# First mixer: the head means from fp32r high and low parts of the squares

## The chip, the cores and the metric

The kernel runs on one core of one Trainium2 chip. The metric is the device time of one execution in microseconds, with the inputs and outputs in device memory. The core has a matrix engine (TensorE, here PE), VectorE (DVE), ScalarE (ACT), GpSimd (POOL) and queues for DMA transfers (SyncE, SP).

## The reference, cut to what matters

Three layers on 512 tokens of width 1024; the first one's mixer is concerned. `h` is the normed input, all in fp32:

```
z = h @ w_in -> gq, gk, gv, gr, glr, sq, sk, sv
# gated linear attention, 4 heads of 128 values
log_a = log_sigmoid(glr @ w_alpha2 + b_alpha) / 16
o_gla = rms_norm(gla_chunked(gq, gk, gv, log_a), gla_norm) * silu(gr)
# window attention, 8 heads of 64, 2 key heads
sq = rms_norm(sq, q_norm); sk = rms_norm(sk, k_norm)
o_swa = swa_sink_attention(sq, sk, sv, sinks)
x = x + concat(o_gla, o_swa) @ w_out
# rms_norm(x, g) = x * rsqrt(mean(x * x) + 1e-6) * g, the mean over one head
```

## The kernel before

Activations stand transposed, features on the 128 partitions and the 512 tokens along a row: a tile is 128x512. Each large product is made of three fp32r products: high parts, and high by low both ways. `three` issues them at lines 2054, 2055 and 2056. ScalarE makes a weight's high part (`split_hi`, line 858), VectorE its low part as the difference (`split_lo`, line 1396). A unit is the product for one tile of outputs: 8 blocks of 3 matmuls. In each engine the program is one stream of instructions in a fixed order; semaphores tie the streams together, and an engine that waits lets nothing past.

The first mixer (`mix_a`, one function for each engine) runs between the last 13 of the 19 units of the input projection. `beside` issues blocks of these units between the mixer's own products, on ACT and DVE the splits and the scaling of a finished unit (`evacuate`, line 1431). The mixer has a head part, and then 19 steps `k`, one for each pair of a head tile `t` and a query block `b` (16 pairs), and three to run out. In step `k` PE does the transposes of pair k-2 (line 2278), the products with the values of pair k-3 (2291), the odd work that the table `MISC_A` puts there, the scores of pair k+1 (2266), and 2 to 4 blocks. The scores wait until DVE has taken the row maxima (1805) of the pair before; the exponentials on ACT (1196) wait for the maxima; POOL scales.

Nine norms are made in this order: `NORMS = ["sk", "sq0", "sq1", "sq2", "sq3", 0, 1, 2, 3]`, numbers 0 to 8 below; the last four are those of the gated heads. For norm i:

- ACT: `squared(i)` (line 1140; for the gated heads line 1222, followed by a copy of the tile, 1224) writes the squares to `sq[:, i % 2, :]`.
- PE: `mean(i, bank)` (line 2252) multiplies them with a constant matrix: `blk64` (1/64 in the two blocks of a head) for i < 5, `ones` (1/1024) for the rest, so that each partition holds the mean of its head.
- ACT: `rooted` takes the logarithm (1148) and the exponential (1151), that is the reciprocal root.
- DVE: `normed` (1749) multiplies.

Operands of a mean are plain fp32. The trace holds two matmul records for each such product, one record for one of fp32r.

Means 0 and 1 stand ahead of the mixer's products for the gate (2359, whose result DVE takes at 1756), mean 2 after 20 further blocks, with six blocks and the first scores behind it. Mean 3 is in step 4, mean 4 in step 8, means 5 and 6 in step 9, means 7 and 8 in step 14. On DVE the head part has the decay's chain: three products of 128x1024 (1782, 1785, 1788) follow each other, the first waiting for an exponential of ACT (1177), and behind them come the scaling of a unit, a split and `normed(2)`. The products of line 2291 for a new head tile wait for the low part of the former one's output (`ol`, DVE line 1840), which is ordered behind the norms of its step.

Of the kernel before, what the change touches and what calls it, by code (L numbers as in the profile page):

```python
# [27 lines left out]
P = 128  # L28
S = 512
# [95 lines left out]
def build(nc, xT, vecs, conv, sinks, w_alpha2, pe, cmp_w1, cmp_w2, weights, yT, flow=FLOW):  # L125
# [6 lines left out]
    with ctx:  # L132
        def sb(name, shape, dt=f32, where=ctx):
            return where.enter_context(nc.sbuf_tensor(name, shape, dt))

        def sem(name):
# [7 lines left out]
        hhi = sb("hhi", [P, KD * S], f32r)  # L144
        hlo = sb("hlo", [P, KD * S], f32r)
        rstd = sb("rstd", [P, S])
        sq = sb("sq", [P, 3, S])
        sumsq = sq[:, 2, :]
        ident = sb("ident", [P, P])
# [50 lines left out]
        fcA = sb("fcA", [P, 32], f32, ma)  # L200
        pT = sb("pT", [P, 2, 2, 2, P], f32, ma)
        rst2 = sb("rst2", [P, 2, S], f32, ma)
        ma.close()

        mb = ExitStack()
# [80 lines left out]
        stored = sem("stored")  # L286

        A = {k: sem("a_" + k) for k in (
            "svT", "svT_c", "nsq", "nms", "nln", "nrstd", "nq", "bias", "zero", "logit", "logit_b", "lsig",
            "decay", "rest", "eb", "enb", "ed", "qe", "ke", "kd", "kdT_c", "masked", "gvT_c", "st", "oc",  # L290
            "misc", "s", "m", "p", "rec", "scaled", "t", "tc", "pv", "sig", "og", "ohi", "olo")}
        B = {}
# [98 lines left out]
        def wlow(n):  # L391
# [6 lines left out]
            if n in KEPT:  # L398
# [32 lines left out]
        MISC_A_NO = {(kind, i): n for n, (kind, i) in enumerate((m[1], m[2]) for m in MISC_A if m[1] != "nm")}  # L431

        def arow(name):
            return tile(zsq, int(name[2])) if name[:2] == "sq" else tile(za, ROW_A[name])
# [393 lines left out]
        def _(act):  # L828
# [302 lines left out]
            def mix_a():  # L1131
                p = "in_a"

                def squared(i):

                    name = NORMS[i]
                    if i >= 2:
                        act.wait_ge(A["nms"], i - 1)
                    act.wait_ge(evac[p], UNIT_A[name] + 1)
                    act.activation(sq[:, i % 2, :], arow(name), ACT.Square).then_inc(A["nsq"], 1)  # L1140

                def rooted(i, bank):

# [8 lines left out]

                squared(0)
                squared(1)
                rooted(0, 4)
                rooted(1, 5)
                act.wait_ge(A["svT"], 1)
# [23 lines left out]
                for k in range(STEPS_A):  # L1181
                    if 0 <= k - 2 < len(PAIRS_A):
                        j = k - 2
                        n = min(PAIRS_A[j][1] + 1, 2)
                        if j >= 2:

                            act.wait_ge(A["pv"], j - 1)
                        act.wait_ge(A["t"], j + 1)
                        act.activation(pT[:, j % 2, :, 2 - n:2, :],
                                       ps[:, 2 + j % 2, :].rearrange("p (g j q) -> p g j q", g=2, q=P)[:, :, 2 - n:2, :],  # L1190
                                       ACT.Copy).then_inc(A["tc"], 1)
                    for s in (2 * k, 2 * k + 1) if k < len(PAIRS_A) else []:
                        w = P * min(PAIRS_A[k][1] + 1, 2)
                        part = pA[:, s % 6, 2 * P - w:2 * P + 1]
                        act.wait_ge(A["m"], s + 1)
                        act.activation(part, part, ACT.Exp, scale=-1.0, bias=nmA[:, s:s + 1], accum_out=smA[:, s:s + 1]
                                       ).then_inc(A["p"], 1)
                    for u in ended(p, k):
                        beside(p, u)
                    if k >= 6 and k % 4 == 2:  # L1200

                        t = k // 4 - 1
                        act.wait_ge(A["pv"], 4 * t + 4)
                        act.activation(tile(oh, 4 + t), ps[:, 4, :], ACT.Copy).then_inc(A["ohi"], 1)
                    if k == 3:
                        squared(3)
                    if k == 7:
                        squared(4)
                    for kind, i, banks in misc_a_at(k):
                        if kind in ("kt", "gv", "o"):  # L1210
                            act.wait_ge(A["misc"], MISC_A_NO[kind, i] + 1)
                        if kind == "kt":
                            act.activation(tile(kdT, i), ps[:, banks[0], :], ACT.Copy).then_inc(A["kdT_c"], 1)
                        if kind == "gv":
                            act.activation(tile(gvT, i), ps[:, banks[0], :], ACT.Copy).then_inc(A["gvT_c"], 1)
                        if kind == "nm":
                            rooted(i, banks[0])
                        if kind == "o":
                            for hh in range(2):
                                h = 2 * i + hh  # L1220
                                act.wait_ge(A["nms"], 4 + h)
                                act.activation(sq[:, (5 + h) % 2, :], ps[:, banks[hh], :], ACT.Square).then_inc(A["nsq"], 1)
                                act.wait_ge(A["gvT_c"], h + 1)
                                act.activation(tile(za, ZGV + h), ps[:, banks[hh], :], ACT.Copy).then_inc(A["oc"], 1)
                for u in finished_at(p, STEPS_A - 1):
# [166 lines left out]
        def _(dve):  # L1392
# [343 lines left out]
            def mix_a():  # L1736
                p = "in_a"

                def normed(i):
# [7 lines left out]
                    else:  # L1747
                        dve.wait_ge(evac[p], UNIT_A[name] + 1)
                    dve.scalar_tensor_tensor(out=out, in0=out, scalar=col(gain), in1=rst2[:, i % 2, :],
                                             op0=ALU.mult, op1=ALU.mult).then_inc(A["nq"], 1)  # L1750

                gk, gq = za[:, ZGK * S:ZGK * S + 2 * S], za[:, ZGQ * S:ZGQ * S + 2 * S]
                dve.wait_ge(ld_vec, 48)
                for t in range(2):
# [16 lines left out]
                for t in range(2):  # L1771
# [15 lines left out]
                dve.wait_ge(evac[p], UNIT_A["gq1"] + 1)  # L1787
                dve.scalar_tensor_tensor(out=gq, in0=gq, scalar=HD ** -0.5, in1=eb[:, :], op0=ALU.mult,
                                         op1=ALU.mult).then_inc(A["qe"], 1)
                beside(p, 9)  # L1790
                dve.wait_ge(evac[p], 10)
                dve.memset(ps[:, 0:2, 2 * P:2 * P + 1], 0.0).then_inc(A["zero"], 1)
# [3 lines left out]
                for k in range(STEPS_A):  # L1796
# [12 lines left out]
                    if 0 <= k - 1 < len(PAIRS_A):  # L1809
                        j = k - 1  # L1810

                        dve.wait_ge(A["p"], 2 * j + 2)
                        dve.reciprocal(fcA[:, 2 * j:2 * j + 2], smA[:, 2 * j:2 * j + 2]).then_inc(A["rec"], 1)
                    for u in ended(p, k):
                        evacuate(p, u, 0)
                    for kind, i, banks in misc_a_at(k):
# [19 lines left out]
                    if k >= 6 and k % 4 == 2:  # L1836

                        t = k // 4 - 1
                        dve.wait_ge(A["ohi"], t + 1)
                        dve.tensor_tensor(tile(ol, 4 + t), ps[:, 4, :], tile(oh, 4 + t).bitcast(f32), ALU.subtract  # L1840
                                          ).then_inc(A["olo"], 1)
                    for u in ended(p, k):
                        n = FIRST[p] + u + 2
                        split_lo(n, 0)
# [205 lines left out]
        def _(pe_):  # L2050
# [195 lines left out]
            def mix_a():  # L2246
                p = "in_a"

                def mean(i, bank):

                    pe_.wait_ge(A["nsq"], i + 1)
                    pe_.matmul(ps[:, bank, :], blk64[:, :] if i < 5 else ones[:, :], sq[:, i % 2, :], start=True, stop=True
                               ).then_inc(A["nms"], 1)

                def scores(k):

# [484 lines left out]
```

## Time and profile before

| | |
|---|---|
| median of 3 runs | 1655.83 us (1655.77 to 1656.39) |
| profiled execution, time | 1656.2 us |
| its span, first to last instruction | 1654.5 us |
| PE busy | 1626.6 us (98%), 8090 matmul records |
| DVE busy | 878.7 us (53%) |
| ACT busy | 709.3 us (43%) |
| POOL busy | 181.4 us (11%) |

The head part of the first mixer runs from about 49 to 76 us of the span, its steps to about 170 us. Times in the rows are microseconds from the span's start. A timeline merges instructions of one line; where it names a mean duration or several records, the start is that of the first. Matmul ends are modelled and overlap the next start, so a matmul's cost is read from start to start. A bracket tells how long the engine sat idle before and which instruction ended that.

### The profile page before, as it was taken

What the parts mean: (1) busy time and instruction counts of PE and PEld (TensorE: products, weight loads), DVE (VectorE), ACT (ScalarE), POOL (GpSimd) and SP (SyncE); (2) the same over time, 40 slices, a digit from 0 to 9 for tenths busy, and PEclk for the clock granted to TensorE, in tenths of its full rate; (3) what the DMA queues carried; (4) which work ended last, traced back from release to release, by engine and by line L of the source; (5) the groups of instructions that cost most, each with busy time, mean ns of one, the idle gap of its engine ahead of it and who ended that gap; (6) DMA issues with size and microseconds to landing.
All of it is one profiled execution on the core that took longest, in us unless ns stands there. A gap on an engine that the chain in (4) does not pass through costs nothing.

```text
span 1654.5 us, 22402 instructions
## 1 busy us (share of the span) xinstructions
PE 1626.6 (98%) x8090; PEld 1350.5 (82%) x8090; DVE 878.7 (53%) x1472; ACT 709.3 (43%) x1210; POOL 181.4 (11%) x257
## 2 busy tenths in 40 slices
PE   8999999999999999999899999999999999999997
PEld 7777788888888888888787888888898888888887
DVE  5634567777743356666756544443238644444233
ACT  4545454444432226676756332232237522323231
POOL 2012000000000032444513000002001200000001
PEclk9999999999999999999999999999999999999999
DMA  5211223322333252121112323233331232333331
GB/s 182 88 41 39 90 89 102 101 89 92 98 102 102 90 130 71 45 65 52 52 61 81 95 96 101 90 101 97 94 115 53 64 101 89 101 95 95 102 102 52
DMA packets 57158, 144.87 MB, mean 88 GB/s; under 512 B 14160, under 2 KB 20976, under 8 KB 57088
## 3 DMA queue, kind: packets, MB, share of 16 engines
q1 hardware_dynamic: 55680, 141.58, 27.4%
q0 software_dynamic: 688, 1.26, 0.4%
q10 hardware_dynamic: 720, 1.10, 0.2%
q8 instruction: 44, 0.72, 0.2%
q14 instruction: 26, 0.21, 0.0%
HBM read 138.67 MB, written 2.10 MB: 85 GB/s over the span
## 4 chain that ended last, share of the span: by engine, by line
PE 93%; ACT 3%; DVE 2%; issue 1%; POOL 0%; DVEq 0%; ACTq 0%; POOLq 0%
PE ps L2054 26%; PE ps L2055 26%; PE ps L2056 26%; PE ps L2155 1%; PE ps L2153 1%; PE ps L2154 1%; PE ps L2223 1%; PE ps L2467 1%; PE ps L2452 1%; PE ps L2505 1%; PE ps L2453 1%; PE ps L2213 1%; PE ps L2626 0%; PE ps L2291 0%; PE ps L2266 0%
## 5 line engine op out<-in xcount | busy, mean ns | idle before, releaser
L2054 PE MATMUL ps<-hhi,whi 128*128 128x512 f32 x1392 | 549.4, 395 | 0.6 <-DVE hlo L2010 0.4
L2056 PE MATMUL ps<-hhi,wlo 128*128 128x512 f32 x1392 | 543.0, 390 | 0.0
L2055 PE MATMUL ps<-hlo,whi 128*128 128x512 f32 x1392 | 543.0, 390 | 0.0
L1396 DVE TENSOR_TENSOR wlo<-raw,whi 128x1024 fp32r<-128x1024 f32 x226 | 276.8, 1225 | 444.6 <-ACT whi L858 441.6
L858 ACT ACTIVATE whi<-raw 128x1024 fp32r<-128x1024 f32 x239 | 252.8, 1058 | 512.1 <-PE ps L2056 512.0
L2054 PEld LDWEIGHTS ps<-hhi,whi 128*128 128x128 f32 x1392 | 261.9, 188 | 62.8 <-issue 8.2
L2056 PEld LDWEIGHTS ps<-hhi,wlo 128*128 128x128 f32 x1392 | 261.7, 188 | 55.3
L2055 PEld LDWEIGHTS ps<-hlo,whi 128*128 128x128 f32 x1392 | 262.0, 188 | 53.3 <-issue 1.2
L2054 PE MATMUL ps<-ahi,whi 128*128 128x512 f32 x432 | 168.0, 389 | 0.0
L2055 PE MATMUL ps<-alo,whi 128*128 128x512 f32 x432 | 168.0, 389 | 0.0
L2056 PE MATMUL ps<-ahi,wlo 128*128 128x512 f32 x432 | 168.0, 389 | 0.0
L923 ACT ACTIVATE ahi<-gated 128x512 f32 (+1 forms) x66 | 41.7, 632 | 148.1 <-DVE gated L1519 148.1
L1490 DVE TENSOR_TENSOR pre<-ps,rstd 128x512 f32<-128x512 f32 x132 | 90.0, 683 | 21.7 <-ACT rstd L1080 14.0
L2054 PEld LDWEIGHTS ps<-ahi,whi 128*128 128x128 f32 x432 | 81.1, 188 | 16.9
L2056 PEld LDWEIGHTS ps<-ahi,wlo 128*128 128x128 f32 x432 | 81.1, 188 | 16.9
L2055 PEld LDWEIGHTS ps<-alo,whi 128*128 128x128 f32 x432 | 81.1, 188 | 16.7
L1521 DVE TENSOR_TENSOR alo<-gated,ahi 128x512 f32 (+1 forms) x66 | 45.7, 692 | 59.3 <-ACT ahi L923 59.3
L1302 ACT ACTIVATE pth<-ps 128x128 fp32r<-128x128 f32 (+3 forms) x96 | 36.7, 433 | 40.3 <-PE ps L2467 39.7
L717 POOL DMA_DIRECT2D cw<-cmp_w x4 | 3.4, 854 | 419.8 <-PE ps L2056 419.8
L1957 DVE TENSOR_TENSOR ptl<-ps,pth 128x128 fp32r<-128x128 f32 (+3 forms) x96 | 42.9, 485 | 11.9 <-ACT pth L1302 11.6
L1412 DVE TENSOR_TENSOR sq<-sq 128x512 f32<-128x512 f32 x42 | 28.9, 688 | 35.6 <-ACT sq L896 25.8
L912 ACT ACTIVATE cvt<-pre,convw 128x512 f32<-128x512 f32 x44 | 35.4, 807 | 28.8 <-DVE pre L1490 28.8
(381 smaller groups left out, 2083.7 us busy)
## 6 DMA issues: line engine op xcount, KB each, us to landing
raw<-w_up_b SPq DMA_DIRECT2D x88, 512.0 KB, 3.4
raw<-w_up_a SPq DMA_DIRECT2D x44, 512.0 KB, 3.5
raw<-w_in_b SPq DMA_DIRECT2D x23, 512.0 KB, 3.5
raw<-w_in_a SPq DMA_DIRECT2D x19, 512.0 KB, 3.5
raw<-w_down_b SPq DMA_DIRECT2D x16, 512.0 KB, 3.5
raw<-w_out_a SPq DMA_DIRECT2D x8, 512.0 KB, 3.5
raw<-w_down_a SPq DMA_DIRECT2D x8, 512.0 KB, 3.5
raw<-w_out_b SPq DMA_DIRECT2D x8, 512.0 KB, 3.4
```

The lines of the kernel that those rows point to most:

```text
L858: act.activation(whigh(n), raw_of(n), ACT.Copy).then_inc(hi_done, 1)
L912: act.activation(cvt[:, s, :], pre[:, s, :], ACT.Identity, bias=convw[:, bass.ds(3 * 2 * KF + c + fi, 1)], scale=convw[:, bass.ds(2 * 2 * ...
L923: act.activation(tile(ahi, f + fi), gated[:, :], ACT.Copy).then_inc(k["ahi"], 1)
L1302: act.activation(pth[:, j % 2, 0:n, s % 2, :], ps[:, 2 + s % 2, 0:n * P].rearrange("p (j q) -> p j q", q=P), ACT.Copy).then_inc(B["hi"], 1)
L1396: dve.tensor_tensor(wlow(n), raw_of(n), whigh(n).bitcast(f32), ALU.subtract).then_inc(lo_done, 1)
L1412: dve.tensor_tensor(sumsq[:, :], sumsq[:, :], sq[:, m % 2, :], ALU.add).then_inc(sq_used, 1)
L1490: dve.tensor_tensor(pre[:, u % 2, :], ps[:, u % 4, :], rstd[:, :], ALU.mult).then_inc(evac[p], 1)
L1521: dve.tensor_tensor(tile(alo, f + fi), gated[:, :], tile(ahi, f + fi).bitcast(f32), ALU.subtract).then_inc(k["alo"], 1)
L1957: dve.tensor_tensor(ptl[:, j % 2, 0:n, s % 2, :], ps[:, 2 + s % 2, 0:n * P].rearrange("p (j q) -> p j q", q=P), pth[:, j % 2, 0:n, s % 2, ...
L2054: pe_.matmul(out, wh, hi, start=start, stop=False)
L2055: pe_.matmul(out, wh, lo, start=False, stop=False)
L2056: return pe_.matmul(out, wl, hi, start=False, stop=stop)
```

## The change

Each mean's squares are written twice by ACT: as fp32, and as fp32r (`sqr`), the high part. DVE subtracts the two and writes the low part as fp32r (`sq_low`) over the fp32 squares, whose memory it shares. PE multiplies high and low part with an fp32r copy of the constant, in two accumulating products in place of one fp32 product. ACT makes the two fp32r constants (`blk64r`, `onesr`) once. The means wait for the low part (semaphore `nql`) in place of the squares (`nsq`). The order of the means on PE is unchanged. DVE's `squared_low(i)` is put into its stream at fixed places: 0 and 1 at the start of the mixer, 2 behind the third of the three long products (`qe`), 5 in step 8 ahead of the unit's scaling, and 3, 4, 6 and 7 with 8 at steps 3, 7, 8 and 13, each ahead of that step's `split_lo`.

```diff
@@ -144,6 +144,9 @@
         hhi = sb("hhi", [P, KD * S], f32r)
         hlo = sb("hlo", [P, KD * S], f32r)
         rstd = sb("rstd", [P, S])
+        over_sq = ExitStack()
+        sq_low = sb("sq_low", [P, 2, S], f32r, over_sq)
+        over_sq.close()
         sq = sb("sq", [P, 3, S])
         sumsq = sq[:, 2, :]
         ident = sb("ident", [P, P])
@@ -200,6 +203,8 @@
         fcA = sb("fcA", [P, 32], f32, ma)
         pT = sb("pT", [P, 2, 2, 2, P], f32, ma)
         rst2 = sb("rst2", [P, 2, S], f32, ma)
+        sqr = sb("sqr", [P, 2, S], f32r, ma)
+        means = sb("means", [P, 2 * P], f32r, ma)
         ma.close()
 
         mb = ExitStack()
@@ -286,7 +291,7 @@
         stored = sem("stored")
 
         A = {k: sem("a_" + k) for k in (
-            "svT", "svT_c", "nsq", "nms", "nln", "nrstd", "nq", "bias", "zero", "logit", "logit_b", "lsig",
+            "svT", "svT_c", "nsq", "nqh", "nql", "nconst", "nms", "nln", "nrstd", "nq", "bias", "zero", "logit", "logit_b", "lsig",
             "decay", "rest", "eb", "enb", "ed", "qe", "ke", "kd", "kdT_c", "masked", "gvT_c", "st", "oc",
             "misc", "s", "m", "p", "rec", "scaled", "t", "tc", "pv", "sig", "og", "ohi", "olo")}
         B = {}
@@ -429,6 +434,14 @@
                   (9, "nm", 5, [7]), (9, "nm", 6, [5]), (10, "gv", 3, [7]), (11, "cs", 1, [5, 7]),
                   (13, "o", 1, [5, 7]), (14, "nm", 7, [5]), (14, "nm", 8, [7])]
         MISC_A_NO = {(kind, i): n for n, (kind, i) in enumerate((m[1], m[2]) for m in MISC_A if m[1] != "nm")}
+
+        def square_hi(i):
+            return sqr[:, i % 2, :]
+
+        def square_lo(i):
+            return sq_low[:, i % 2, :]
+
+        blk64r, onesr = means[:, 0:P], means[:, P:2 * P]
 
         def arow(name):
             return tile(zsq, int(name[2])) if name[:2] == "sq" else tile(za, ROW_A[name])
@@ -1138,6 +1151,7 @@
                         act.wait_ge(A["nms"], i - 1)
                     act.wait_ge(evac[p], UNIT_A[name] + 1)
                     act.activation(sq[:, i % 2, :], arow(name), ACT.Square).then_inc(A["nsq"], 1)
+                    act.activation(square_hi(i), arow(name), ACT.Square).then_inc(A["nqh"], 1)
 
                 def rooted(i, bank):
 
@@ -1152,6 +1166,9 @@
 
                 squared(0)
                 squared(1)
+                act.wait_ge(const_a, 1)
+                act.activation(blk64r, blk64[:, :], ACT.Copy).then_inc(A["nconst"], 1)
+                act.activation(onesr, ones[:, :], ACT.Copy).then_inc(A["nconst"], 1)
                 rooted(0, 4)
                 rooted(1, 5)
                 act.wait_ge(A["svT"], 1)
@@ -1220,6 +1237,7 @@
                                 h = 2 * i + hh
                                 act.wait_ge(A["nms"], 4 + h)
                                 act.activation(sq[:, (5 + h) % 2, :], ps[:, banks[hh], :], ACT.Square).then_inc(A["nsq"], 1)
+                                act.activation(square_hi(5 + h), ps[:, banks[hh], :], ACT.Square).then_inc(A["nqh"], 1)
                                 act.wait_ge(A["gvT_c"], h + 1)
                                 act.activation(tile(za, ZGV + h), ps[:, banks[hh], :], ACT.Copy).then_inc(A["oc"], 1)
                 for u in finished_at(p, STEPS_A - 1):
@@ -1749,6 +1767,15 @@
                     dve.scalar_tensor_tensor(out=out, in0=out, scalar=col(gain), in1=rst2[:, i % 2, :],
                                              op0=ALU.mult, op1=ALU.mult).then_inc(A["nq"], 1)
 
+                def squared_low(i):
+
+                    dve.wait_ge(A["nsq"], i + 1)
+                    dve.wait_ge(A["nqh"], i + 1)
+                    dve.tensor_tensor(square_lo(i), sq[:, i % 2, :], square_hi(i).bitcast(f32), ALU.subtract
+                                      ).then_inc(A["nql"], 1)
+
+                squared_low(0)
+                squared_low(1)
                 gk, gq = za[:, ZGK * S:ZGK * S + 2 * S], za[:, ZGQ * S:ZGQ * S + 2 * S]
                 dve.wait_ge(ld_vec, 48)
                 for t in range(2):
@@ -1787,6 +1814,7 @@
                 dve.wait_ge(evac[p], UNIT_A["gq1"] + 1)
                 dve.scalar_tensor_tensor(out=gq, in0=gq, scalar=HD ** -0.5, in1=eb[:, :], op0=ALU.mult,
                                          op1=ALU.mult).then_inc(A["qe"], 1)
+                squared_low(2)
                 beside(p, 9)
                 dve.wait_ge(evac[p], 10)
                 dve.memset(ps[:, 0:2, 2 * P:2 * P + 1], 0.0).then_inc(A["zero"], 1)
@@ -1811,6 +1839,8 @@
 
                         dve.wait_ge(A["p"], 2 * j + 2)
                         dve.reciprocal(fcA[:, 2 * j:2 * j + 2], smA[:, 2 * j:2 * j + 2]).then_inc(A["rec"], 1)
+                    if k == 8:
+                        squared_low(5)
                     for u in ended(p, k):
                         evacuate(p, u, 0)
                     for kind, i, banks in misc_a_at(k):
@@ -1839,6 +1869,8 @@
                         dve.wait_ge(A["ohi"], t + 1)
                         dve.tensor_tensor(tile(ol, 4 + t), ps[:, 4, :], tile(oh, 4 + t).bitcast(f32), ALU.subtract
                                           ).then_inc(A["olo"], 1)
+                    for i in {3: [3], 7: [4], 8: [6], 13: [7, 8]}.get(k, []):
+                        squared_low(i)
                     for u in ended(p, k):
                         n = FIRST[p] + u + 2
                         split_lo(n, 0)
@@ -2248,9 +2280,11 @@
 
                 def mean(i, bank):
 
-                    pe_.wait_ge(A["nsq"], i + 1)
-                    pe_.matmul(ps[:, bank, :], blk64[:, :] if i < 5 else ones[:, :], sq[:, i % 2, :], start=True, stop=True
-                               ).then_inc(A["nms"], 1)
+                    pe_.wait_ge(A["nconst"], 2)
+                    pe_.wait_ge(A["nql"], i + 1)
+                    weight = blk64r if i < 5 else onesr
+                    pe_.matmul(ps[:, bank, :], weight, square_hi(i), start=True, stop=False)
+                    pe_.matmul(ps[:, bank, :], weight, square_lo(i), start=False, stop=True).then_inc(A["nms"], 1)
 
                 def scores(k):
 
```

## Rows read from the trace of the kernel before

**Rows 1.** The page: chain that ended last, share of the span by engine.

```profile
PE 93%; ACT 3%; DVE 2%; issue 1%; POOL 0%; DVEq 0%; ACTq 0%; POOLq 0%
```

**Rows 2.** Timeline of PE, 46 to 58 us: start us, us, engine line, count.

```profile
49.44 1.88 PE L2252 MATMUL ps<-sq,blk 128*128 128x512 f32 x4
51.26 1.12 PE L2359 MATMUL ps<-za,wal 16*128 16x512 f32 x2
52.31 0.50 PE L2054 MATMUL ps<-hhi,whi 128*128 128x512 f32 x1
52.64 0.40 PE L2055 MATMUL ps<-hlo,whi 128*128 128x512 f32 x1
52.88 0.39 PE L2056 MATMUL ps<-hhi,wlo 128*128 128x512 f32 x1
```

**Rows 3.** Timeline of PE, 62 to 76 us.

```profile
70.33 1.02 PE L2252 MATMUL ps<-sq,blk 128*128 128x512 f32 x2
...
71.42 0.40 PE L2055 MATMUL ps<-hlo,whi 128*128 128x512 f32 x1
```

**Rows 4.** Timeline of DVE, 36 to 76 us.

```profile
69.85 1.23 DVE L1782 TENSOR_TENSOR kd<-za,kd 128x1024 f32<-128x1024 f32 x1 [0.78 <-ACT kd L1177]
...
73.46 0.68 DVE L1431 TENSOR_TENSOR za<-ps,rstd 128x512 f32<-128x512 f32 x1
```

**Rows 5.** Timeline of PE, 104 to 134 us.

```profile
118.86 1.12 PE L2252 MATMUL ps<-sq,blk 128*128 128x512 f32 x2
119.92 0.70 PE L2266 MATMUL ps<-za,zsq 64*128 64x256 f32 x4
...
131.95 0.70 PE L2266 MATMUL ps<-za,zsq 64*128 64x256 f32 x4 [0.42 <-DVE nmA L1805]
```

**Rows 6.** Timeline of PE, 142 to 184 us.

```profile
153.18 1.98 PE L2252 MATMUL ps<-sq,ones 128*128 128x512 f32 x4
...
158.62 0.44 PE L2291 MATMUL ps<-pT,svT 128*64 128x128 f32 x4
```

**Rows 7.** Timeline of ACT, 36 to 76 us.

```profile
50.50 0.69 ACT L1148 ACTIVATE rst<-ps,epsc 128x512 f32<-128x512 f32 x1 [4.58 <-PE ps L2252]
...
66.81 0.61 ACT L1140 ACTIVATE sq<-zsq 128x512 f32<-128x512 f32 x1
...
68.76 1.06 ACT L1177 ACTIVATE kd<-kd 128x1024 f32<-128x1024 f32 x1 [0.38 <-DVE kd L1774]
```

**Rows 8.** Timeline of ACT, 142 to 184 us.

```profile
150.42 0.60 ACT L1222 ACTIVATE sq<-ps 128x512 f32<-128x512 f32 x1 [1.93 <-PE ps L2340]
...
151.39 0.60 ACT L1222 ACTIVATE sq<-ps 128x512 f32<-128x512 f32 x1
...
153.04 0.50 ACT L1196 ACTIVATE pA<-pA,nmA 128x257 f32<-128x257 f32 x1
```

**Rows 9.** Timeline of DVE, 142 to 184 us.

```profile
148.53 1.22 DVE L1396 TENSOR_TENSOR wlo<-raw,whi 128x1024 fp32r<-128x1024 f32 x1 [2.36 <-ACT whi L858]
150.89 0.43 DVE L1805 CUSTOM_DVE_ANT_0 pA<-ps,biasA 128x257 f32<-128x257 f32 x1 [1.14 <-PE ps L2266]
...
157.79 0.68 DVE L1840 TENSOR_TENSOR ol<-ps,oh 128x512 fp32r<-128x512 f32 x1
```

**Rows 10.** Waits, 44 to 165 us: total, times, longest us.

```profile
DVE la L1756 <- PE ps L2359: 9.5, 2, 6.4
```

**Rows 11.** Timeline of ACT, 104 to 134 us.

```profile
120.03 0.60 ACT L1222 ACTIVATE sq<-ps 128x512 f32<-128x512 f32 x1 [4.21 <-PE ps L2252]
```

**Rows 12.** Timeline of DVE, 104 to 134 us.

```profile
123.64 0.75 DVE L1749 SCALAR_TENSOR_TENSOR zsq<-zsq,vec,rst 128x512 f32<-128x512 f32 x1 [8.06 <-ACT rst L1151]
124.31 0.42 DVE L1805 CUSTOM_DVE_ANT_0 pA<-ps,biasA 128x257 f32<-128x257 f32 x1
```

**Rows 13.** Windows of 20 us: busy us by engine, PEclk, DMA share, GB/s.

```profile
640.00:660.00 20.00, 18.71 (x90) 15.59 (x91) 12.31 (x46) 12.29 (x38) 9.87 (x13) 0.83 0.21 53
```

**Rows 14.** Waits of PE over the whole span.

```profile
PE ps L2452 <- DVE nmB L1941: 5.8, 16, 1.4
PE ps L2189 <- POOL ident L680: 4.6, 1, 4.6
```

## Prediction

> **What bounds the kernel now.** I read the page first: which engine the chain that ended last runs over. It is TensorE (PE) for 93% [rows 1]: what takes a matmul off PE is worth its time, unless an operand comes late. The change sits in the first mixer, so I then read the timelines of PE, ScalarE (ACT) and VectorE (DVE) from 44 to 170 us side by side. The reader is to see three things there. A mean costs PE two half-rate passes [rows 2, 3]. Mean 2 stands on PE at 70.33, long before DVE is through with the long products of the gates, the first at 69.85 [rows 3, 4]. And at two places PE waits for DVE: before the scores at 131.95 (0.42 us idle) and before the products at 158.62 [rows 5, 6], each after a mean whose root runs over ACT and DVE. Anything put on ACT or DVE ahead of these is on the path.
>
> **Prices.** From mean 2's start to that of the second product after it are 1.09 us; one product is 0.24 (52.64 to 52.88), so an f32 mean holds PE 0.86 [rows 2, 3]. Products of fp32r start 0.23 to 0.24 apart, the first behind f32 work 0.33 [rows 2]. So the new pair costs 0.33 + 0.23 = 0.56. Means 0 and 1 took 1.82 (49.44 to 51.26); now 0.33 + 3 x 0.23 = 1.02, and up to 0.1 for the way back to f32: saved 0.75. Mean 2 saves 0.30. A mean inside the loop took 1.06 to the next score (118.86 to 119.92) [rows 5]; 0.2 of that may be the scores' own weight load and stay: saved 0.3 to 0.5, I take 0.4. The pairs 5, 6 and 7, 8 save about 0.8 each. Everything together is 0.75 + 0.30 + 2 x 0.4 + 2 x 0.8 = 3.45 us, if nothing waits. The second square holds ACT 0.49 (150.42 to 151.39 is a square and a copy) [rows 8]. A subtraction is of the form of line 1840, 0.68 long, and holds DVE 0.61, half of the 1.22 of a 128x1024 one [rows 9].
>
> **Means 0 and 1: a gain.** Squares, copies of the constants and subtractions fall before 49.44. ACT stood idle 4.58 us before the root at 50.50, and DVE up to 6.4 us for the products of line 2359 [rows 7, 10]. The two extra squares and two copies (128 columns each, at most a square) need 4 x 0.49 = 2.0 us, two subtractions 2 x 0.61 = 1.2 us: hidden. Without that cover they would cost their own length, 3.2 us. The products of line 2359 start 0.75 early, and DVE's additions, which waited for them, go with them; so does all that hangs on them up to 70 us.
>
> **Mean 2: a wait.** ACT does the second square behind the one at 66.81. Behind it are queued two exponentials; the later, at 68.76, had 0.38 us of idle time before it [rows 7] and comes 0.05 to 0.15 late against its old distance, and DVE's product at 69.85 waits for it [rows 4]. The subtraction is put behind the third long product. DVE was free of that at 73.46 [rows 4]; now 73.46 - 0.75 + 0.05 = 72.76, and the low part is there at 72.76 + 0.68 + 0.05 = 73.49. PE comes to the mean at 70.33 - 0.75 = 69.58 and stands 3.9 us, with nothing else allowed past. Queued behind it are 18 products and all of the loop. Mean 2 starts 3.16 late and saves 0.30: PE is 2.86 late. ACT and DVE gain slack, PE alone sets the pace from there, so nothing takes this back.
>
> **Mean 3.** The subtraction in step 3 stands before the unit's split and waits for ACT; the split used to wait for the unit's high part alone, and two squares and a subtraction now lie between: 0.49 + 0.60 + 0.61 = 1.7 us, and the row maxima behind the split are as much later. PE asks for these only behind 12 products (2.8 us at 0.23), transposes and the mean, so I cost it at nothing; without that cover it is up to 1.7. PE: 2.86 - 0.4 = 2.46 late. Subtraction 4 (step 7) has the same form and DVE idle around it; subtraction 5 too.
>
> **Steps 8 to 10: a dearer chain.** From mean 4 to the scores at 131.95 the chain left PE: square and copy on ACT (120.03, released by the mean), exponentials, the root, line 1749 on DVE at 123.64, maxima at 124.31, and again ACT and DVE up to the scores [rows 5, 11, 12]. The mean now ends 0.40 earlier (0.33 + 0.39 against 1.12 long), the second square adds 0.49, subtraction 6 stands between 123.64 and 124.31 and adds 0.60: +0.69. What means 4, 5 and 6 save on PE is lost in the wait at these scores. PE: 2.46 + 0.69 = 3.15 late.
>
> **Steps 13 and 14: a new wait.** ACT has square 150.42, second square, copy, square, second square: the last starts at 150.42 + 4 x 0.485 = 152.36 and ends at 152.96. DVE's subtraction 8 waits for it (153.0 to 153.6). Queued behind are the split of line 1396, which was at 148.53, now 153.6 to 154.75, and the maxima of pair 14, at 150.89 before, now 154.75 [rows 8, 9]. The exponentials need these: 154.75 + 0.43 + 0.01 = 155.19 in place of 153.04, 2.15 late [rows 8]. Everything after them on ACT and DVE, the two roots, line 1749 twice and line 1840 at 157.79, was a gapless chain from there to the products at 158.62, which had just been waiting for it: 2.15 late [rows 6, 9]. Mean 7 and 8 themselves (153.18) have their operands within 0.1 us, and their 0.8 is lost in the wait. PE: 3.15 + 2.15 = 5.3 late, and what follows is released by PE.
>
> **Sum.** Profiled execution: 1654.5 span and 1.7 around it, 1656.2. With +5.3: 1661.5. The median of the runs shown is 0.4 below the profiled one, so I forecast 1661.1 us. Own range: mean savings 0.3 or 0.5 each, subtraction held at 0.59 to 0.69, the exponential 0.05 or 0.15 late: 1660.2 to 1662.2.
>
> **The clock.** Between 640 and 660 us the clock granted to PE was 0.83 on the mean, with PE busy 18.71 of 20 us [rows 13]: it stood at the lower of its two levels (1.2 of 2.4 GHz) for a part of them. (1 - 0.83) x 20 = 3.4 us of full clock were lost, without a long wait there. Outside the start, the longest wait of PE for another engine in the whole trace is 1.4 us [rows 14]; the new one is 3.9. The fall costs between nothing and 3.4 us. I take nothing, because dense products stand on both sides of the wait, and price the other as a rival. The Trainium skill (TensorE: Matmul & The Clock Gate, section "Why this matters for your kernels") says that a long idle gap between bursts of matmuls drops the clock; by that rule the fall comes in this wait, against this change; the trace has a fall, but no such wait to show it by.
>
> **Rivals.** *The clock falls in the wait for mean 2.* For: the row above, where less brought it down. Against: the dense work around it. A loss of 3.4 is a low stretch of 6.8 us; what of it lies in the wait is free, at most 3.9, so (6.8 - 3.9) / 2 = 1.5 to 3.4 is left, about 2.3: 1663.4. *The later fall goes away.* The fall near 640 us came without a long wait, so the same work 5 us later may not bring it. Up to 3.4 comes back, less what DVE's and ACT's own chains held up there anyway; I take 2.3: 1661.1 - 2.3 = 1658.8, no measurable change. *Only mean 2's wait counts.* If ACT's and DVE's additions in steps 8 to 14 are covered after all, PE is 2.86 late and gets up to 2 x 0.4 + 2 x 0.8 = 2.4 back: 1656.3 to 1658.7, no change. Against: chains without gaps. *Faster.* The one mechanism is that the subtractions come in time, so that the two passes fewer are PE's gain: 1655.83 - 3.45 = 1652.4. It decides at mean 2: DVE would have to reach subtraction 2 at 68.9 in place of 72.76, and this needs three 1.1 us products out of its way; they are in its queue, in order.
>
> **Chances.** Forecast 0.55; clock falls in the wait 0.22; later fall gone 0.10; only mean 2 0.09; faster 0.04. About 0.2%, 3.3 us, is what a measurement of this kernel can tell from no change: 1652.5 to 1659.1. So slower 0.80 (forecast, clock, a part of the others), same 0.16, faster 0.04. The range takes the first three in: 1658.3 to 1664.6.
>
> **What would show it.** PE idle some 3.9 us before line 2252's third mean, released by DVE's subtraction; if it is under 1 us, the step on mean 2 is wrong. Nine new pairs at about 0.23 to 0.33 apart in place of 18 half-rate passes. Idle PE of 1.5 to 2 us before the scores of step 10 and before the products of step 15, where 0.42 and next to nothing were; DVE's split and maxima of step 13 behind a subtraction that waits for ACT. Granted clock 1.00 from 60 to 180 us. Behind 180 us the same sequence, 5.3 us later. The prediction is wrong if the clock moves by more than 2 us in sum, or if the loop absorbs one of the three delays.

## The result, and the profile after

The changed kernel takes 1664.60 us (median of 5 runs, 1663.74 to 1665.13) against 1655.83 us (1655.54 to 1656.39): the ratio is 1.0055, 95% interval 1.0044 to 1.0065, so 7 to 11 us slower. Forecast were 1661.1 and at most 1664.6. The profiled execution has a span of 1662.0 us, 7.5 more than before.

The page of the changed kernel, its first part and the chain by engine, answering to [rows 1]:

```profile
PE 1625.7 (98%) x8090; PEld 1351.2 (81%) x8090; DVE 884.4 (53%) x1481; ACT 713.6 (43%) x1221; POOL 181.0 (11%) x257
...
PE 92%; ACT 3%; DVE 3%; issue 2%; POOL 0%; DVEq 0%; ACTq 0%; POOLq 0%
```

PE is busy 0.9 us less than before (1625.7 against 1626.6) in a span that is 7.5 longer, so it stands still 8.4 us more. The busy time alone does not show the clock: cheaper means and slower products are both in it. The waits of PE over the whole span say where it stands (engine and line, waited for; total, times, longest, in us); of [rows 14] the start's 4.6 and the second mixer's are still there, and three lines are new or grown, by 8.3 us together (the second one was 0.4 before):

```profile
PE ps L2286 <- DVE sq_low L1774: 4.2, 2, 3.8
PE ps L2300 <- DVE nmA L1833: 2.7, 2, 1.7
PE ps L2325 <- DVE ol L1870: 1.8, 1, 1.8
```

Timeline of PE around mean 2, answering to [rows 3]. Lines 2086 to 2088 are the three products of a block, 2286 and 2287 the mean's pair, 2300 the scores:

```profile
69.44 0.39 PE L2088 MATMUL ps<-hhi,wlo 128*128 128x512 f32 x1
73.67 0.47 PE L2286 MATMUL ps<-sqr,means 128*128 128x512 f32 x1 [3.84 <-DVE sq_low L1774]
73.97 0.39 PE L2287 MATMUL ps<-sq_low,means 128*128 128x512 f32 x1
...
74.93 0.63 PE L2086 MATMUL ps<-hhi,whi 128*128 128x512 f32 x1
75.36 0.63 PE L2087 MATMUL ps<-hlo,whi 128*128 128x512 f32 x1
...
80.03 0.49 PE L2300 MATMUL ps<-za,zsq 64*128 64x128 f32 x4
```

The last product before the mean starts at 69.44; PE then sits idle 3.84 us until DVE's subtraction. The pair starts 0.30 apart and costs what the fp32r products around it do. From 74.9 the same products start 0.43 apart, not 0.23. DVE in the same stretch, answering to [rows 4]:

```profile
69.23 1.23 DVE L1809 TENSOR_TENSOR kd<-za,kd 128x1024 f32<-128x1024 f32 x1 [0.80 <-ACT kd L1194]
...
71.70 1.22 DVE L1815 SCALAR_TENSOR_TENSOR za<-za,eb 128x1024 f32<-128x1024 f32 x1
72.84 0.68 DVE L1774 TENSOR_TENSOR sq_low<-sq,sqr 128x512 fp32r<-128x512 f32 x1
```

The subtraction (line 1774) stands behind the long products and starts at 72.84. Windows of the changed kernel (us; PE, PEld, DVE, ACT and POOL busy, then the granted clock):

```profile
72.00:76.00 4.00, 2.33 (x8) 1.92 (x9) 3.52 (x6) 1.32 (x2) 0.00 (x0) 0.86 0.00 0
76.00:80.00 4.00, 4.00 (x13) 2.90 (x12) 0.54 (x1) 0.00 (x0) 0.00 (x0) 0.72 0.40 131
164.00:168.00 4.00, 2.19 (x10) 1.70 (x11) 2.28 (x8) 1.86 (x6) 1.47 (x3) 0.88 0.00 0
168.00:172.00 4.00, 4.00 (x21) 2.89 (x20) 0.69 (x1) 1.33 (x2) 0.69 (x2) 0.70 0.00 0
640.00:660.00 20.00, 18.92 (x102) 15.78 (x100) 12.03 (x46) 11.95 (x38) 5.09 (x8) 0.91 0.20 52
```

The clock is below 1 in every row. Before, it was 1.00 in the first four of these windows and 0.83 in the last [rows 13]. At (1 - clock) x length, 1.68 us of full clock are lost at each of the first two places (0.56 + 1.12, and 0.48 + 1.20); at 640 us 1.8 are lost where it was 3.4.

The two places in the loop, PE, answering to [rows 5, 6]:

```profile
123.09 0.50 PE L2286 MATMUL ps<-sqr,means 128*128 128x512 f32 x1
...
123.74 0.70 PE L2300 MATMUL ps<-za,zsq 64*128 64x256 f32 x4
...
136.87 0.70 PE L2300 MATMUL ps<-za,zsq 64*128 64x256 f32 x4 [1.68 <-DVE nmA L1833]
```

```profile
158.13 0.50 PE L2286 MATMUL ps<-sqr,means 128*128 128x512 f32 x1
...
160.60 0.70 PE L2300 MATMUL ps<-za,zsq 64*128 64x256 f32 x4 [1.03 <-DVE nmA L1833]
...
165.81 0.44 PE L2325 MATMUL ps<-pT,svT 128*64 128x128 f32 x4 [1.83 <-DVE ol L1870]
...
168.26 0.63 PE L2086 MATMUL ps<-hhi,whi 128*128 128x512 f32 x1
```

The scores of step 10 wait 1.68 us for the row maxima, the products of step 15 1.83 for the low part of line 1870. DVE and ACT in steps 13 and 14, answering to [rows 8, 9]:

```profile
158.03 0.69 DVE L1774 TENSOR_TENSOR sq_low<-sq,sqr 128x512 fp32r<-128x512 f32 x1 [0.78 <-ACT sqr L1240]
158.63 1.22 DVE L1414 TENSOR_TENSOR wlo<-raw,whi 128x1024 fp32r<-128x1024 f32 x1
159.77 0.42 DVE L1833 CUSTOM_DVE_ANT_0 pA<-ps,biasA 128x257 f32<-128x257 f32 x1
...
164.99 0.68 DVE L1870 TENSOR_TENSOR ol<-ps,oh 128x512 fp32r<-128x512 f32 x1
```

```profile
157.29 0.63 ACT L1240 ACTIVATE sqr<-ps 128x512 fp32r<-128x512 f32 x1
...
160.23 0.51 ACT L1213 ACTIVATE pA<-pA,nmA 128x257 f32<-128x257 f32 x1 [1.54 <-DVE nmA L1833]
```

DVE waits 0.78 us for ACT's second square (157.29), subtracts, splits, and only then takes the maxima for which the exponential at 160.23 has waited 1.54.

Start of the same work in both profiled executions, from the timelines of PE (ACT for the loading of the Silu table):

| work | before | after | later by |
|---|---|---|---|
| mean 0 | 49.44 | 49.50 | 0.06 |
| mean 2 | 70.33 | 73.67 | 3.34 |
| first scores | 75.40 | 80.03 | 4.63 |
| mean 4 | 118.86 | 123.09 | 4.23 |
| scores in step 10 | 131.95 | 136.87 | 4.92 |
| mean 7 | 153.18 | 158.13 | 4.95 |
| products in step 15 | 158.62 | 165.81 | 7.19 |
| Silu table on ACT | 171.30 | 180.10 | 8.80 |
| first compression product, second mixer | 626.7 | 635.5 | 8.8 |
| end | 1654.5 | 1662.0 | 7.5 |

### The profile page after: what moved, and what is told of

Its sections match the earlier page's. It is cut to its first block, busy times and chain, and to the rows that moved or that the text cites. A ratio compares the mean times of both kernels' runs of the same rounds, so it can differ in the third digit from the quotient of the medians.

```text
span 1662.0 us, 22433 instructions
## 1 busy us (share of the span) xinstructions
PE 1625.7 (98%) x8090; PEld 1351.2 (81%) x8090; DVE 884.4 (53%) x1481; ACT 713.6 (43%) x1221; POOL 181.0 (11%) x257
## 4 chain that ended last, share of the span: by engine, by line
PE 92%; ACT 3%; DVE 3%; issue 2%; POOL 0%; DVEq 0%; ACTq 0%; POOLq 0%
PE ps L2086 26%; PE ps L2087 25%; PE ps L2088 25%; PE ps L2187 1%; PE ps L2185 1%; PE ps L2186 1%; PE ps L2255 1%; PE ps L2501 1%; PE ps L2486 1%; PE ps L2539 1%; PE ps L2487 1%; PE ps L2245 1%; PE ps L2660 0%; PE ps L2325 0%; PE ps L2300 0%
```

## The experiments

Ten kernels were run, each against the kernel before on the same chip; the medians of that kernel there were 1655.73 (first four), 1655.76 (next four) and 1656.21 us (last two). One profile was taken of each. Where a profile and the median of its kernel tell different things, both are given: two executions of one kernel can differ by 1 to 3 us.

### Subtraction 2 ahead of the long products

```diff
                 dve.memset(state[:, :, 0, :], 0.0).then_inc(A["st"], 1)
+                squared_low(2)
                 dve.wait_ge(A["ed"], 1)
...
-                squared_low(2)
                 beside(p, 9)
```

> Subtraction 2 moved ahead of the three long products, into DVE's idle 0.8 us. Theory A (waits and clock falls): the wait for mean 2 (3.84 us) is gone and with it the clock fall behind it; PE is 1.05 us early at the first scores where it was 4.63 late, 0.8 early at the scores of step 10, 1.5 late at the products of step 15; with or without the second fall (1.7) and the changed fall near 640 us: 1657 to 1660 us. Theory B (only the wait counts, the clock loss comes anyway): 1664.6 - 3.9 = 1660.7 or more. Theory C (means were slow in themselves): near 1664.

Measured: 1659.78 us (1657.41 to 1661.11), ratio 1.0021 (1.0012 to 1.0031). PE's timeline around the mean and the first scores, and DVE's behind the moved subtraction:

```profile
70.51 0.39 PE L2286 MATMUL ps<-sqr,means 128*128 128x512 f32 x1
...
75.58 0.49 PE L2300 MATMUL ps<-za,zsq 64*128 64x128 f32 x4 [0.32 <-DVE ps L1820]
```

```profile
70.03 1.23 DVE L1810 TENSOR_TENSOR kd<-za,kd 128x1024 f32<-128x1024 f32 x1 [0.26 <-ACT kd L1194]
```

No wait before the pair. This execution started its mixer 0.86 later than the one before (50.30 against 49.44 for mean 0), so the first scores at 75.58 are 0.68 early, not 1.05: they wait 0.32 for DVE's zeroing (line 1820). The moved subtraction did not delay that: the first long product behind it still waits 0.26 for ACT. The zeroing itself comes 0.67 earlier, counted from mean 0 (25.17 behind it, before 25.84), but PE comes 1.0 earlier. Behind it everything went as in the changed kernel: 1.68 us of wait at step 10, 1.81 at step 15, and the clock fell there alone (0.79 in 160 to 164 and in 164 to 168 us). One place of one instruction was worth 4.8 us of 8.8. Theory B (1660.7 or more) is out by the windows, where the first fall is gone; the time, 0.9 us below it, would not rule it out, since its interval reaches 1660.9.

### The wait for mean 2 filled

```diff
                 pe_.wait_ge(A["nln"], 1)
+                for n in range(16):
+                    pe_.matmul(ps[:, 4, :], blk64r, square_hi(1), start=True, stop=True)
                 mean(2, 4)
```

> Sixteen products of 128x512 without use (3.6 us) fill the wait for mean 2; nothing else is changed. Theory A: the wait stays as long, the clock does not fall behind it: 1.7 us less, about 1662.9 (1662.2 to 1663.6). Theory B (the fall has another cause, or costs nothing): no change from 1664.6, granted clock below 1 near 75 us again.

Measured: 1662.64 us (1660.73 to 1664.59), ratio 1.0038 (1.0024 to 1.0053). Windows of this kernel, from an execution of 1664.2 us:

```profile
76.00:80.00 4.00, 4.00 (x20) 3.04 (x19) 1.27 (x5) 0.38 (x2) 0.00 (x0) 1.00 0.39 131
...
136.00:140.00 4.00, 4.00 (x14) 2.88 (x11) 1.45 (x6) 1.33 (x4) 1.95 (x4) 0.60 0.40 128
...
168.00:172.00 4.00, 4.00 (x20) 2.91 (x19) 0.69 (x1) 1.11 (x2) 1.03 (x2) 0.64 0.00 0
```

The clock stays at 1.00 after mean 2, which itself is no earlier (74.08, 4.20 behind the filling's start at 70.08). The first scores start 3.42 later than before, with mean 0 0.44 later: 2.98 by the change, against 4.57 without the filling. So the fall behind this wait is from PE standing still in it, and costs 1.6 us. The rows show this and the time alone does not: its interval overlaps that of the changed kernel (1.0044 to 1.0065). In this execution it fell at 137 us instead, behind the wait of step 10, where it had not in the changed kernel's profile.

### Subtractions 7 and 8 behind the maxima

```diff
-                    for i in {3: [3], 7: [4], 8: [6], 13: [7, 8]}.get(k, []):
+                    for i in {3: [3], 7: [4], 8: [6]}.get(k, []):
...
                     if k == 8:
                         squared_low(5)
+                    if k == 14:
+                        squared_low(7)
+                        squared_low(8)
```

> Subtractions 7 and 8 moved from step 13 to step 14, behind the row maxima of pair 14. Theory A: the split and the maxima are back in time, the chain to the products of step 15 is 0.6 late for the two squares of ACT in place of 2.2; the wait of 1.83 us there shrinks to about 1.4, the second fall is gone or not: 1.6 to 3.3 less, 1661.3 to 1663.0. Theory B (that chain is bound by the squares on ACT alone): 1664 to 1665.

Measured: 1662.54 us (1660.15 to 1662.85), ratio 1.0033 (1.0018 to 1.0047). DVE's timeline:

```profile
154.17 1.23 DVE L1414 TENSOR_TENSOR wlo<-raw,whi 128x1024 fp32r<-128x1024 f32 x1 [2.36 <-ACT whi L871]
156.53 0.43 DVE L1833 CUSTOM_DVE_ANT_0 pA<-ps,biasA 128x257 f32<-128x257 f32 x1 [1.14 <-PE ps L2303]
...
158.72 0.76 DVE L1774 TENSOR_TENSOR sq_low<-sq,sqr 128x512 fp32r<-128x512 f32 x1 [0.74 <-ACT sqr L1240]
...
164.01 0.69 DVE L1873 TENSOR_TENSOR ol<-ps,oh 128x512 fp32r<-128x512 f32 x1
```

Split and maxima wait for nobody's square any more. From mean 7 to the products of step 15 are 6.01 us (158.83 to 164.84); they were 5.44 before and 7.68 in the changed kernel: +0.57 and +2.24. The wait is 1.17 us, and no fall followed it. The fall at mean 2 was larger in this execution:

```profile
72.00:76.00 4.00, 2.40 (x6) 1.95 (x7) 3.25 (x5) 1.14 (x2) 0.00 (x0) 0.50 0.00 0
76.00:80.00 4.00, 4.00 (x14) 3.14 (x13) 0.75 (x1) 0.18 (x1) 0.00 (x0) 0.65 0.39 131
```

That is 3.4 us of clock lost in place of 1.7, with a wait of 3.81 us. So the time falls into theory A's range, but what was saved at step 15 (1.67 by the rows, and the 1.7 of the fall) is partly hidden by the other fall.

### A wait alone, in the kernel before

```diff
                 pe_.wait_ge(A["nln"], 1)
+                pe_.wait_ge(A["qe"], 1)
                 mean(2, 4)
```

> The kernel before, where mean 2 on PE also waits for the third long product of DVE (nothing of the change in it). Theory A: wait of 3.1 us at mean 2 and a clock fall of 1.7 behind it, then up to 1.3 given back or taken near 640 us: 1659 to 1662, likeliest 1660.6. Theory B (a wait does not bring the clock down): 1658.9. Rival that slack takes the wait back: 1656.

Measured: 1661.21 us (1659.64 to 1661.61), ratio 1.0029 (1.0019 to 1.0039). PE's timeline and the windows:

```profile
73.44 2.05 PE L2252 MATMUL ps<-sq,blk 128*128 128x512 f32 x2 [3.17 <-issue]
```

```profile
72.00:76.00 4.00, 2.56 (x4) 1.46 (x5) 3.14 (x5) 0.47 (x1) 0.00 (x0) 0.54 0.01 2
76.00:80.00 4.00, 4.00 (x12) 3.09 (x12) 0.75 (x1) 0.84 (x2) 0.00 (x0) 0.60 0.39 131
```

Nothing of the change is in this kernel. A wait of 3.17 us cost 5.9 at the first scores (81.34 against 75.40) and 5.5 in the time: (0.46 + 0.40) x 4 = 3.4 us of clock were lost in this execution, a part of it inside the wait, which ended at 73.44: from 72 to 73 us the granted clock was 0.68, from 73 on 0.50. A wait on PE alone brings the clock down.

### All late subtractions moved

The first and third edit together, and subtraction 6 behind the maxima of step 9.

```diff
+                squared_low(2)
                 dve.wait_ge(A["ed"], 1)
...
+                    if k == 9:
+                        squared_low(6)
+                    if k == 14:
+                        squared_low(7)
+                        squared_low(8)
...
-                    for i in {3: [3], 7: [4], 8: [6], 13: [7, 8]}.get(k, []):
+                    for i in {3: [3], 7: [4]}.get(k, []):
```

> The whole change, with subtraction 2 ahead of the long products, subtraction 6 behind the row maxima of step 9, and 7 and 8 behind those of step 14. Theory A: PE is 0.7 to 1.05 early at the first scores, 1.1 to 1.4 before mean 4, some 1.0 to 1.3 at the scores of step 10 (square +0.49, mean -0.40), and 0.4 to 0.7 at the products of step 15 (two squares, +0.6); no wait over 1.5 us in the mixer, so no extra fall of the clock: 1654.8 to 1656.2. Theory B (the change is dearer by something other than the places of the subtractions): 1658 or more.

Measured: 1655.34 us (1653.68 to 1656.29), ratio 1.0000 (0.9990 to 1.0009). PE's rows at the two places:

```profile
131.08 0.70 PE L2305 MATMUL ps<-za,zsq 64*128 64x256 f32 x4 [0.39 <-DVE nmA L1833]
...
158.37 0.44 PE L2330 MATMUL ps<-pT,svT 128*64 128x128 f32 x4 [1.18 <-DVE ol L1875]
```

From mean 4 to the scores of step 10 are 13.17 us (117.91 to 131.08) against 13.09 before (118.86 to 131.95) and 13.78 in the changed kernel. The longest wait in the mixer is 1.18 us, before the products of step 15; the clock is 1.00 throughout the mixer. All of the change is in here: two squares, nine pairs, nine subtractions. With them in other places it costs nothing and brings nothing that the time shows. PE is 0.87 early at step 10 and 0.25 at step 15: what means 0 to 4 gain, the second squares take back in steps 13 and 14.

### Means 0 to 4 alone

Means 5 to 8 in fp32 from one square each, as before; subtraction 2 early.

```diff
                 def mean(i, bank):
 
+                    if i >= 5:
+                        pe_.wait_ge(A["nsq"], i + 1)
+                        pe_.matmul(ps[:, bank, :], ones[:, :], sq[:, i % 2, :], start=True, stop=True
+                                   ).then_inc(A["nms"], 1)
+                        return
```

> High and low parts for means 0 to 4 alone, subtraction 2 ahead of the long products; means 5 to 8 in fp32 as before, with one square each. Theory A: 0.7 to 1.05 early at the first scores, 0.4 more after mean 3, 0.4 more by mean 4's earlier end, and nothing lost behind it: 1.5 to 1.9 early to the end, 1653.9 to 1654.6. Theory B (ACT's or DVE's added work in steps 3 and 7 costs too): 1655 to 1656.

Measured: 1654.35 us (1653.85 to 1654.80), ratio 0.9992 (0.9983 to 1.0001). Mean 0 starts at 49.40, first scores at 74.67 (0.73 early), mean 4 at 117.71 (1.15 early), scores of step 10 at 130.39 (1.56 early), and 1.5 early at the second mixer (625.2 against 626.7): the gain of means 0 to 4 is kept. The rows show it; the interval of the ratio just reaches 1.

### High parts alone

The low parts are left out: one square, one product, no subtraction, so the means are those of rounded squares.

```diff
-                    act.activation(sq[:, i % 2, :], arow(name), ACT.Square).then_inc(A["nsq"], 1)
...
-                squared_low(0)
-                squared_low(1)
...
-                    pe_.wait_ge(A["nql"], i + 1)
+                    pe_.wait_ge(A["nqh"], i + 1)
```

> The low parts are left out: ACT writes the fp32r squares alone, PE makes one product for each mean, DVE subtracts nothing. PE's gain without ACT's and DVE's work. Theory A: means 0 and 1 save 1.26, mean 2 0.63, mean 3 0.5 to 0.7, mean 4 as much on the chain; means 5 to 8 lose their gain in the waits: about 3.0 early at the end, 1652.5 to 1653.3. If the waits were not there it would be 5.5 or more: 1650.3.

Measured: 1654.32 us (1652.34 to 1656.02), ratio 0.9991 (0.9981 to 1.0000). A miss by 1 us or more. PE's rows at the two waits, and the windows between:

```profile
74.50 0.49 PE L2290 MATMUL ps<-za,zsq 64*128 64x128 f32 x4 [0.60 <-DVE ps L1815]
```

```profile
129.78 0.70 PE L2290 MATMUL ps<-za,zsq 64*128 64x256 f32 x4 [1.67 <-DVE nmA L1828]
```

```profile
128.00:132.00 4.00, 2.33 (x10) 1.58 (x9) 2.78 (x10) 2.06 (x6) 1.09 (x2) 0.84 0.40 131
132.00:136.00 4.00, 4.00 (x25) 3.00 (x27) 1.16 (x6) 0.44 (x1) 1.09 (x2) 0.73 0.02 4
```

The first scores wait 0.60 for the zeroing and are 0.9 early in place of 1.9. At step 10 PE is 2.17 early, but has waited 1.67 us, and the clock fell: 0.64 + 1.08 = 1.7 us lost. With less work on PE the waits grow. In this execution PE was 1.54 us early at mean 4 (117.32) and 0.58 at mean 7 (152.60): what one product in place of two passes saved at means 4 to 6 was less than the grown wait and the fall behind it took. The median is still 1.4 us below that of the kernel before, with an interval that ends at 1.0000.

### ACT's second squares alone

```diff
                                 act.activation(sq[:, (5 + h) % 2, :], ps[:, banks[hh], :], ACT.Square).then_inc(A["nsq"], 1)
+                                act.activation(sqr[:, (5 + h) % 2, :], ps[:, banks[hh], :], ACT.Square)
```

> The kernel before, where ACT squares the four gated heads a second time into a tile that nobody reads. It measures ACT's part alone. Theory A: +0.49 at the scores of step 10 and +0.6 at the products of step 15, no clock fall: 1.1 more, 1656.6 to 1657.2. Theory B (ACT's slack hides the squares): 1655.8.

Measured: 1656.81 us, ratio 1.0005 (0.9996 to 1.0015). Mean 4 to the scores of step 10: 13.58 (118.63 to 132.21), +0.49. Mean 7 to the products of step 15: 6.02 (153.47 to 159.49), +0.58. The rows show both terms; the time alone can't tell 1.05 us from nothing.

### All three waits filled

The changed kernel with the filling of mean 2's wait, and this function called with (7, 7) before the scores of step 10 and with (8, 8) before the products of step 15:

```diff
+                def warm(n, count):
+                    pe_.wait_ge(A["nln"], n)
+                    for c in range(count):
+                        pe_.matmul(ps[:, 5, :], blk64r, square_hi(1), start=True, stop=True)
```

> The changed kernel with all three longer waits filled by products of 128x512 without use: 16 before mean 2, 7 before the scores of step 10, 8 before the products of step 15. Theory A (the waits cost what the sum of the prediction says, 5.3, the rest of the loss is clock falls behind them): no granted clock below 1 between 44 and 200 us, products of step 15 about 5.4 to 5.7 late, 1660.3 to 1661.6, likeliest 1661.0. Theory B (the excess over 5.3 is not the clock): 1662.6 as with one filled wait, or 1664.6. Rival that the filling itself delays: more than 1662.6.

Measured: 1660.85 us (1660.08 to 1661.56), ratio 1.0031 (1.0019 to 1.0042). The windows where it had fallen:

```profile
76.00:80.00 4.00, 4.00 (x21) 3.00 (x20) 1.18 (x5) 0.48 (x3) 0.00 (x0) 1.00 0.41 131
...
136.00:140.00 4.00, 4.00 (x30) 3.07 (x32) 2.15 (x7) 1.47 (x5) 1.67 (x4) 1.00 0.32 125
...
168.00:172.00 4.00, 4.00 (x26) 3.11 (x25) 1.23 (x1) 1.72 (x3) 0.00 (x0) 1.00 0.20 28
```

The waits are as long as in the changed kernel, by their chains: 13.78 us from mean 4 to the scores of step 10 (121.59 to 135.37) and 7.69 from mean 7 to the products of step 15 (156.63 to 164.32), there 13.78 and 7.68. All instructions of the change are there too. Only the clock is kept, and 3.75 us are gone by the medians; the intervals of the two ratios do not overlap. PE is 5.70 late at the products of step 15, with mean 0 0.20 later: 5.5 by the change. What is left over the kernel before is 4.6 us by its median in this comparison and 5.1 by the ratio: the waits.

### The zeroing ahead of the split

Means 0 to 4 alone, and:

```diff
-                beside(p, 9)
+                evacuate(p, 9, 0)
                 dve.wait_ge(evac[p], 10)
                 dve.memset(ps[:, 0:2, 2 * P:2 * P + 1], 0.0).then_inc(A["zero"], 1)
+                split_lo(FIRST[p] + 11, 0)
```

> As the kernel with means 0 to 4 alone, and DVE's zeroing of a column of the scores' banks ahead of the split that it stood behind. Theory A: the wait of 0.33 us before the first scores is gone, and all behind it is as much earlier: 1654.0 (1653.6 to 1654.4). Rival: the split, 0.06 us later, is asked for by PE: no gain, 1654.35.

Measured: 1653.55 us (1652.20 to 1654.19), ratio 0.9984 (0.9975 to 0.9993). The fastest kernel of the study, just below theory A's range.

```profile
69.63 0.39 PE L2287 MATMUL ps<-sqr,means 128*128 128x512 f32 x1
...
74.31 0.49 PE L2301 MATMUL ps<-za,zsq 64*128 64x128 f32 x4
```

No wait before the scores (74.31, 1.09 early, mean 0 at 49.44 as before); step 10 at 130.05, 1.90 early, the second mixer at 624.8, 1.9 early.

## Why the prediction was wrong

**The waits: right, term by term.** Mean 2: PE was to stand 3.9 us and be 2.86 late; it stood 3.84, and with the clock kept was 2.98 late. Means 0 and 1: forecast 0.75 saved, measured 0.72 (the last product before mean 2 starts at 69.44 where it was 70.10, with mean 0 0.06 later). Mean 3: forecast 0.40 saved at no cost; from the first scores to mean 4 the delay went from 4.63 to 4.23. Steps 8 to 10: forecast +0.69, measured 4.92 - 4.23 = +0.69; the second square is 0.49 of it (ACT's squares alone), and the subtraction's 0.6 less the mean's 0.4 the rest (with subtraction 6 moved, the chain is +0.08). Steps 13 and 14: forecast +2.15, measured 7.19 - 4.95 = +2.24, of which 0.57 stays when the subtractions are moved. With the clock kept they add up to 5.5 us, where the sum said 5.3 and 1661.1 us, and the kernel with filled waits measured 1660.85.

**The step that failed is the clock.** "I take nothing, because dense products stand on both sides of the wait" was wrong: the clock fell behind the wait for mean 2 (1.68 us lost) and again behind that of step 15 (1.68), at which I had not looked for it at all. The rival with the clock took one fall, 2.3, and 1663.4; two of 1.7 and the waits give 5.3 + 3.4 = 8.7, and 8.8 is what PE was late at 626 us. So a fall was priced too high (2.3 for 1.7) and counted once in place of twice. The median lies at the upper end of my range, and by the ratio (1655.83 x 1.0055 = 1664.9) beyond it. That these falls come from PE standing still is shown twice, by filling the waits (they go, 3.75 us with them) and by a wait alone in the kernel before (it comes). At mean 2 the clock fell in all three profiles with the long wait unfilled (3.84, 3.81 and 3.17 us) and in neither of the two with it filled. The Trainium skill (TensorE: Matmul & The Clock Gate, section "Why this matters for your kernels") says that a long idle gap between bursts of matmuls drops the clock; the traces agree for these three waits: the clock fell behind the first and within the other two. That rule deserved the larger chance.

**The rivals.** *The later fall goes away*: in part. 1.7 us of clock were lost at 640 us in place of 3.4 (1.8 by the rounded row above), and the delay went from 8.8 to 7.5. But the loss there is not a fixed one: over the twelve profiled kernels it was 3.4 us in four, 1.7 in seven and nothing in one (all late subtractions moved), and the kernel before itself ranged over 3.1 us (1653.82 to 1656.91 in 33 runs). So I don't count this as an effect of the change. That the medians differ by 8.8 and the profiled executions by 7.5 may come from these falls; no run separates the two. *Only mean 2's wait counts* and *faster* are ruled out by the rows of this kernel. Where DVE has the subtraction in time the change does gain, for means 0 to 4: 1.56 us at step 10, and 1.90 with the zeroing moved as well, which is no part of the change.

**Open.** Waits shorter than these are not all alike. Behind that of step 15, when it was 1.8 us long, the clock fell in three profiles of three (the changed kernel, subtraction 2 early, first wait filled); at 1.17 to 1.34 us never, in three. Behind that of step 10, 1.66 to 1.68 us long, it fell in two of five. Nor is a long wait needed: near 640 us the clock fell in eleven of twelve profiles, where no single wait of PE for another engine was over 0.70 us. In the kernel before it was at 0.88 from 641 to 642 us and at 0.50 in the microsecond behind it, around this wait:

```profile
641.65 0.45 PE L2452 MATMUL ps<-kst,qst 128*128 128x256 f32 x1 [0.38 <-DVE nmB L1941]
```

What decides between falling and not was not settled, and one profile for each kernel gives no frequency.

## What to carry to other kernels

A cheaper instruction on the engine that sets the pace can be worth nothing, or cost time, if its operand is made by one more step in another engine's fixed order: look up in that engine's timeline what stands ahead of the new step, and what is queued behind it. Where the sum gives PE a new wait, price the clock too, even between dense products: here it fell at all three waits over 3 us and behind five of eight of 1.66 to 1.83 us, a fall cost 1.7 us or more, about as much as the shorter waits themselves, and products that nobody reads, issued into the wait, took it away. A short wait is no guarantee against a fall, as the stretch near 640 us shows. An operation added on a chain whose root is already waited for should go behind the next thing that PE asks for, and where the chain has no slack at all (means 5 to 8 here) the old form is the better one.

## What the runs showed of the hardware

The granted clock went to the lower level (0.50 over 75 to 78 us, 1.2 of 2.4 GHz) not only at waits of 3.84, 3.81 and 3.17 us, but behind five of eight waits of 1.66 to 1.83 us too, with dense products on both sides. A fall cost 1.7 us, and about 3.4 at two of the long ones (the wait alone, and the kernel with subtractions 7 and 8 moved, 0.50 and 0.65 in the windows from 72 to 80 us); there it began inside the wait. The same two sizes, 1.7 and 3.4, stand near 640 us. Fewer instructions on PE can lose a part of their gain by this: without the low parts PE was 2.17 us early at step 10, and 1.7 were lost to the clock at once.
